# A two-layer trunk on one core: both layers and TensorE's MLP groups written out, the first two MLP blocks side by side, the rounded part of the weights ahead of their remainder

## What is computed

```python
def _trunk_layer(x, p, l, cond, ctx):
    mod = (cond @ p['w_ada'][l] + p['b_ada'][l]).reshape(cond.shape[0], 1, 6, D_MODEL)
    sh_a, sc_a, gt_a, sh_m, sc_m, gt_m = [mod[:, :, i] for i in range(6)]
    h = _rmsnorm(x, p['norm_mix_w'][l]) * (1.0 + sc_a) + sh_a
    mix, new_ctx = _mixer_sublayer(h, p, l, ctx)
    x = x + gt_a * mix
    h = _rmsnorm(x, p['norm_mlp_w'][l]) * (1.0 + sc_m) + sh_m
    x = x + gt_m * (jnp.square(jax.nn.relu(h @ p['mlp_w1'][l])) @ p['mlp_w2'][l])
    return x, new_ctx
```

## Time and profile before

| | us |
|---|---|
| median of 3 runs | 3024.26 (3023.71 to 3024.54) |
| the profiled execution | 3019.77 |
| its span | 3018.2 |
| TensorE busy in it | 2843.2 (94%) |
| VectorE, ScalarE, GpSimd busy | 1061.4, 798.2, 659.2 |
| last square of layer 1 to last square of layer 2 | 1478 |

### The profile page before, as it was taken

One profiled execution on the slowest core, in us unless ns is written; L12 is line 12 of the kernel. 1 busy time (PEld: TensorE's weight loads), 2 busy tenths in 40 slices (PEclk: granted clock), 3 DMA queues, 4 the chain that ended last, 5 costly groups with the idle time before them and its releaser, 6 DMA issues.

```text
span 3018.2 us, 55846 instructions
## 1 busy us (share of the span) xinstructions
PE 2843.2 (94%) x23136; PEld 2384.0 (79%) x23136; DVE 1061.4 (35%) x1944; ACT 798.2 (26%) x1214; POOL 659.2 (22%) x428
## 2 busy tenths in 40 slices
PE   6999999999999899999989998999999998999997
PEld 3558855887778899999956697568777888999997
DVE  1546613236533411111344474132465233111113
ACT  2131013223321422122221411232233214221222
POOL 0002101221222233333301110021122222333332
PEclk9999999999999999999999999999999999999998
DMA  7110011222124222223330100112221332322222
GB/s 307 35 47 13 3 37 42 81 79 79 64 99 137 80 92 91 92 84 93 98 129 22 43 4 6 59 49 79 79 79 64 128 105 87 98 85 92 88 95 77
DMA packets 56672, 235.54 MB, mean 78 GB/s; under 512 B 6625, under 2 KB 6785, under 8 KB 55137
## 3 DMA queue, kind: packets, MB, share of 16 engines
q1 hardware_dynamic: 53568, 206.67, 20.8%
q0 software_dynamic: 2848, 25.13, 2.2%
HBM read 222.96 MB, written 8.81 MB: 77 GB/s over the span
## 4 chain that ended last, share of the span: by engine, by line
PE 87%; issue 4%; DVE 3%; ACT 3%; POOL 1%; DMA 1%; SPq 0%; POOLq 0%; DVEq 0%; ACTq 0%
PE ps_dense L774 43%; PE ps_dense L767 14%; PE ps_aux L774 4%; PE ps_aux L1350 3%; PE ps_dense L1299 3%; PE ps_aux L1096 2%; PE ps_aux L1076 2%; PE ps_aux L1088 2%; PE ps_aux L1299 1%; PE ps_dense L1376 1%; PE ps_dense L1364 1%; DMA w_ring<-in_w_early 1%; PE ps_dense L797 1%; PE ps_aux L797 1%; POOL w_low L679 1%
## 5 line engine op out<-in xcount | busy, mean ns | idle before, releaser
L679 POOL TENSOR_TENSOR w_low<-w_ring,w_high 128x1024 fp32r<-128x1024 f32 x208 | 512.5, 2465 | 1226.3 <-ACT w_high L1613 1226.3
L774 PE MATMUL ps_dense<-h_high,w_high 128*128 128x320 f32 x2048 | 482.6, 317 | 52.8 <-DVE h_low L2029 22.2
L774 PE MATMUL ps_dense<-h_low,w_high 128*128 128x320 f32 x2048 | 469.0, 310 | 0.0
L774 PE MATMUL ps_dense<-h_high,w_low 128*128 128x320 f32 x2048 | 468.9, 310 | 0.0
L767 PE MATMUL ps_dense<-h_norm,w_ring 128*128 128x512 f32 (+1 forms) x1536 | 432.1, 442 | 18.7 <-ACT h_norm L1638 10.7
L767 PEld LDWEIGHTS ps_dense<-h_norm,w_ring 128*128 128x128 f32 x1536 | 239.1, 195 | 216.3 <-issue 205.2
L774 PEld LDWEIGHTS ps_dense<-h_high,w_high 128*128 128x128 f32 x2048 | 339.5, 189 | 67.7 <-issue 29.9
L1613 ACT ACTIVATE w_high<-w_ring 128x1024 fp32r<-128x1024 f32 x208 | 219.4, 1056 | 569.8 <-PE ps_dense L774 350.6
L774 PEld LDWEIGHTS ps_dense<-h_low,w_high 128*128 128x128 f32 x2048 | 345.0, 189 | 0.0
L774 PEld LDWEIGHTS ps_dense<-h_high,w_low 128*128 128x128 f32 x2048 | 344.8, 189 | 0.0
L774 PE MATMUL ps_dense<-z_high,w_high 128*128 128x320 f32 x1024 | 235.6, 311 | 0.0
(11 more groups left out here) (404 smaller groups left out, 3557.5 us busy)
## 6 DMA issues: line engine op xcount, KB each, us to landing
w_ring<-in_w_mlp SPq DMA_DIRECT2D x128, 512.0 KB, 3.7
w_ring<-in_w_gate SPq DMA_DIRECT2D x64, 640.0 KB, 4.0
w_ring<-in_w_late SPq DMA_DIRECT2D x64, 512.0 KB, 4.7
w_ring<-in_w_early SPq DMA_DIRECT2D x48, 512.0 KB, 3.6
w_ring<-in_w_in SPq DMA_DIRECT2D x48, 512.0 KB, 3.6
w_ring<-in_w_out SPq DMA_DIRECT2D x16, 512.0 KB, 3.7
arena<-in_dft POOLq DMA_DIRECT2D x2, 3264.0 KB, 12.9
par<-in_par POOLq DMA_DIRECT2D x3, 1731.0 KB, 7.6
```

Of the source, the lines that this page charges most:

```text
L679: g.tensor_tensor(w_low[:, n % 2], ring[:, slot, 0:KC, :], w_high[:, n % 2].bitcast(F32), ALU.subtract).then_inc(w_low_in.sem, 1)
L774: last = mm(out[:, s, 0:HALF], w_[:, par_, k, :], x_[:, k, s * HALF:(s + 1) * HALF], start=k == 0 and x_ is x_high and w_ is w_high, stop= ...
```

## The change

What it does:

- The loops over the layers are written out in all five programs, and TensorE's loop over the MLP groups too. The inner loops of the other four stay. Waits on TensorE are then on constants.
- `dense_split` (output projection and MLP) waits for `w_high` only, runs all matmuls on `w_high` first (4 a chunk), then waits for `w_low` and runs the 16 matmuls on it.
- The first two blocks of each layer's MLP run side by side (`first_blocks`): pair of chunks by pair of chunks, all matmuls on `h_high` for block 0 and for block 1, with `w_high` and `w_low`, and then the matmuls on `h_low`, block 0 and block 1.
- ScalarE makes the rounded copy of chunk c directly behind its modulation, and VectorE scales all eight chunks before it makes the first remainder.

```diff
             def dense_split(out, par_, x_high, x_low, low_ready, ready=None):
                 for k in range(KC):
                     if ready:
                         pe.wait_ge(*ready(k))
-                    last = split_tile(out, par_, k, x_high, x_low)
-                if last_of_block:
-                    last.then_inc(block_done.sem, 1)
+                    split_part(out, par_, k, w_high, x_high, k == 0)
+                    split_part(out, par_, k, w_high, x_low)
+                pe.wait_ge(*low_ready)
+                for k in range(KC):
+                    last = split_part(out, par_, k, w_low, x_high, False, k == KC - 1)
+                last.then_inc(block_done.sem, 1)
...
+            def split_part(out, par_, k, w_, x_, first=False, final=False):
+                for s in range(2):
+                    last = mm(out[:, s, 0:HALF], w_[:, par_, k, :], x_[:, k, s * HALF:(s + 1) * HALF], start=first,
+                              stop=final)
+                return last
...
             def out_proj(l):
                 for m in range(KC):
-                    pe.wait_ge(*w_low_in.nth(l, N_GATE + m + 1))
+                    pe.wait_ge(*w_high_in.nth(l, N_GATE + m + 1))
...
+            def first_blocks(l):
+                n = N_GATE + N_OUT
+                pe.wait_ge(*w_low_in.nth(l, n + 2))
+                for kk in range(0, KC, 2):
+                    for b in range(2):
+                        if kk == 0:
+                            pe.wait_ge(*residual.nth(l, 7 + b))
+                        for k in (kk, kk + 1):
+                            if b == 0:
+                                pe.wait_ge(*h_high_in.nth(l, KC + k + 1))
+                            split_part(dense_banks(b), b, k, w_high, h_high, k == 0)
+                            split_part(dense_banks(b), b, k, w_low, h_high)
+                for b in range(2):
+                    for k in range(KC):
+                        if b == 0:
+                            pe.wait_ge(*h_split.nth(l, KC + k + 1))
+                        last = split_part(dense_banks(b), b, k, w_high, h_low, False, k == KC - 1)
+                    last.then_inc(block_done.sem, 1)
...
             def mlp(l):
-                with pe.Fori(0, GROUPS) as g:
+                for g in range(GROUPS):
+                    mlp_group(l, g, g == 0)
...
-            with pe.Fori(0, DEPTH) as l:
+            for l in range(DEPTH):
...
             def modulate(l, which):
                     last.then_inc(h_ready.sem, 1)
-                    if which and c:
-                        high_of_h(l, c - 1)
-                if which:
-                    high_of_h(l, KC - 1)
+                    if which:
+                        high_of_h(l, c)
...
             def norm(l, which):
                 for c in range(KC):
                     v.tensor_tensor(h[:, c], x[:, c], rs[:], ALU.mult).then_inc(x_scaled.sem, 1)
-                    if which and c >= 3:
-                        low_of_h(l, c - 3)
                 if which:
-                    for c in range(KC - 3, KC):
+                    for c in range(KC):
                         low_of_h(l, c)
```

More of the change, by code:

```diff
@@ L584, in _ @@
             pool.wait_ge(const_rest_in.sem, 16)
-            with pool.Fori(0, DEPTH) as l:
+            for l in range(DEPTH):
                 held(pool, *residual.nth(l, 0))
@@ L1979, in _ @@
                 square(0, c, 0)
-            with act.Fori(0, DEPTH) as l:
+            for l in range(DEPTH):
                 chain.l, chain.n = l, 0
@@ L2693, in _ @@
             dve.wait_ge(x_in.sem, 16)
-            with dve.Fori(0, DEPTH) as l:
+            for l in range(DEPTH):
                 chain.l, chain.n = l, 0
```

71 lines of the change are left out of this document (38 added, 33 removed).

## The result

| | before | after |
|---|---|---|
| median of the runs, us | 3023.99 (3022.58 to 3024.54) | 2992.73 (2989.59 to 2996.11) |
| the profiled execution, its span | 3019.77, 3018.2 | 2991.51, 2989.7 |

A forecast was written before the change was run, and what follows sets the result against it. TensorE bounds the kernel, so only its idle and half-clock stretches pay. Terms 12.8 + 3.8 + 7.5 + 3.2 + 1.0 = 28.3 us take the median from 3024.3 to 2996 us; range 2985 to 3006.

The forecast's parts named there:

- Part 1: Start of the output projection: running matmuls on w_high before waiting for w_low gains 12.8 us over two layers, bounds 9.6 and 14.6.
- The other 138 blocks at nothing: Remaining reordered output-projection and MLP blocks: no gain or loss, since the remainder is already hidden behind a block of work.
- Part 2: Start of each MLP: the first two blocks side by side reach the modulation rows earlier, 3.8 us in all.
- if the pace stays 1.72, the gain is 2.8 a layer: Side-by-side MLP start: with ScalarE's copies at 1.72 us a chunk instead of 1.84, 5.6 us in all.
- Part 3: TensorE's MLP group loop written out: the stops at six taken back edges go, 7.5 us.
- Part 4: Layer loops written out: ScalarE's edge, from last square to first scaled chunk, shrinks from 8.22 to 5.04 us, gaining 3.2.
- Part 5: Waits against constants instead of registers, 330 register instructions fewer on TensorE: 1 us, likely upper bound 4.
- A: Rival, chance 0.07: clock stays halved through the side-by-side MLP start, making that term -4 to -5 us; time 3004 to 3005.
- B: Rival, chance 0.05: group-loop edges are cheap or their stops are VectorE's; 4 to 7 us less gain, 3000 to 3003.
- C: Rival, chance 0.05: register instructions matter in small-matmul and engine-chain stages, half of 21 us shows; time 2986, or 2980.
- D: Rival, chance 0.03: slower, because TensorE's straight text must fetch each new page of instructions in time; 3071 us.

## Why the prediction was right, and where it was off

The forecast was 2996 us in a range of 2985 to 3006, and the median is 2992.7. The sum of 28.3 us meets the 28.3 us between the profiled executions, but that is partly luck. Two terms are off by 1.0 and 1.7 us in opposite directions, and between the first dense block and the end of the merge two chance swings of +2.59 and -2.82 us cancelled.

**Part 1 (12.8, measured 12.6).** The 2.0 us pause is 1.83. The open question, whether such a pause halves the clock, got both answers: yes in layer 1 (a gain of 5.64), no in layer 2 (7.00). The forecast had taken 6.4 for both, so that its 12.8 is this near is luck; with the halved clock in neither layer, as in two other profiles, it would be 14.2, and in both, as in one, 11.1. Halved, the clock cost 1.5 us here and not the 2.5 that the forecast took from the long pause. Undoing the order gives 12.35.

**"The other 138 blocks at nothing"** holds where the blocks stand one behind another: the output projection's later blocks and the MLP show no wait for `w_low`. It misses one thing. Block 2 of each MLP, behind the side-by-side pair, would have lost 3.9 us a layer in the old order. Parts 1 and 2 were costed as if each stood alone.

**Part 2 (3.8, measured 2.8).** The mechanism and the sequence were right: TensorE is behind at half clock, catches up and ends on the last copy. The step that was mis-sized is the working from copy 7 on. The pace is 1.86 and not 1.84, the last copy ends 15.0 us behind the start of the modulation and not 14.8, and after its wait TensorE needs 1059.87 - 1053.23 = 6.64 us and not 6.5. These add to 0.4 of the 0.5 us a layer that are missing; the forecast's own times give 1.82, which it rounded up to 1.9. The line "if the pace stays 1.72, the gain is 2.8 a layer" is borne out by the run with late copies (1.39 + 1.13 = 2.5).

**Part 3 (7.5, measured 9.2).** The edges were real, all six, VectorE's label notwithstanding. What was short is the price of a stop. An idle time of 1.15 us counts from the modelled end of the last matmul. But in a running block the next one starts 0.147 us after the last one's start, not at its end 0.31 us after it, and the first pair behind a stop takes 0.56 us instead of 0.46 (the row at 1053.23 above, against the others). That is 0.16 + 0.10 us a stop, 1.6 for six: 7.5 + 1.6 = 9.1. The looped kernels bear it out: idle times of 0.95 + 1.08 and 1.34 + 1.38 us in layer 1, with 0.52 each, give 2.55 and 3.24, and 2.56 and 3.25 were measured.

**Part 4 (3.2, measured 3.0).** 5.05 us at the edge against 5.04 forecast. The clock does halve there, as assumed, and with extra matmuls in the pause the 2.6 us show.

**Part 5 (1.0, too small to be told from nothing).** Four engines' register waits brought back make no stage longer by more than 0.2 us, so the waits' register instructions are hidden. The -0.2 of the table is the rest of the two swings and not a measurement of this part.

**The rivals.** A is refuted: the clock is back at 1.00 after 5.2 us of the side-by-side phase. Stretches and granted clock:

```profile
1040.29:1045.50 5.21, 4.85 (x17) 0.50 0.01 3
1045.53:1052.00 6.47, 5.53 (x37) 1.00 0.00 0
```

B: the edges went with the loop, and came back with it at most places in the text, at one of them for nothing. C: the run with registers shows nothing. D: straight text exposes no fetch. There is no "issue" on the matmul line, and layer 2's MLP takes 451.69 us with its packets as without. But the fear had a true core, since a fetch that is not done in time stops TensorE for up to 3.1 us: in straight text it is done in time, behind a jump it was not.

The median gained 3 us more than the profiles. The runs of one kernel spread over 2 to 13 us, most likely by the half-clock stretches ahead of the end of the merge, and I can't attribute these 3 us further.

## What to carry to other kernels

A loop's back edge on the engine that sets the time has a price that depends on its place in the text (0, 1.3 to 1.8, or 6 us here), so measure each edge in each copy of the loop, since a neighbour's edit can move it. When producer and consumer go chunk by chunk, the time of the last chunk counts and not that of the first: ScalarE's "earlier" copy cost 1.1 us a layer, and making the copies on an engine with time to spare gained 3 us a layer. Where an idle time on TensorE can't be removed, matmuls without a purpose kept its clock here. A reordering that ends a block later must be followed to whoever waits for its buffer. And a pause that may or may not halve the clock is a spread in the forecast, not a value between.

## What the runs showed of the hardware

- A taken branch on TensorE: 0.22 to 0.24 us in one place, 3.3 to 3.9 us in others. The same loop moved by 64 instructions went from 12.06 us for two edges to 0, and there no instruction packet arrived in 245 us.
- A fetch can show twice at one edge: 1.16 us, five matmuls, then 3.14 us, when the loop starts 48 instructions short of the end of a 256-instruction piece.
- A pause of 1.83 us in a dense block was followed by 10 matmuls at full clock and 15 at 1.2 GHz in layer 1, and by none at 1.2 GHz in layer 2 of the same execution.
- 10 matmul records of 512 columns on fp32, 4.46 us in a pause of 5.2, kept the clock at 1.00 for the two dense blocks behind it, 2.6 us less. 16 of them, 7.03 us, did so ahead of the MLP.
- Rounding 128 x 640 takes VectorE 0.48 us and ScalarE 0.74. On ScalarE a copy directly behind the modulation it depends on costs 0.14 us a chunk more than one that follows an independent modulation.
